# A hybrid convolution and attention block on eight cores: output rounds of two tiles, a block finish dealt by step, a later first stage, one jump to each body

## The chip, the cores and the metric

The kernel runs on the eight cores of one Trainium2 chip, as one program without collectives. Each core has its own engines (TensorE, VectorE or DVE, ScalarE or ACT, GpSimd or POOL, SyncE or SP) and DMA queues. The metric is the device time in microseconds of the slowest core. Cores 0 to 3 take one sequence of the batch and cores 4 to 7 the other; core c runs the code of piece c modulo 4.

## What is computed

```python
xn = rmsnorm(x, g_in)                                   # x: (2, 4096, 4096)
proj = xn @ w_in
gB, gC, h, z_conv, c_q, c_kv, k_rope, z_attn = split(proj)
y_conv = gB * causal_short_conv(gC * h, conv_w) * silu(z_conv)        # 2048 channels
q = rmsnorm(c_q) @ w_uq ; k_nope, v = split(rmsnorm(c_kv) @ w_ukv)    # 16 heads, 128 + 64 rotary
attn = chunk_causal_attention(q, k, v)                  # chunks of 64 frames, blocks of 128
y = concat(y_conv, attn * silu(z_attn))
out = rmsnorm(x + y @ w_out, g_final)
```

## The kernel before

`build_core` writes the instruction lists of one piece of the sequence. `PLAN` gives each piece its start, its number of tokens and their groups: piece 0 has 1232 tokens in groups of 360, 360 and 512, piece 1 has 1072 (280, 280, 512), piece 2 has 944 (432, 512), piece 3 has 848 (464, 384). A later piece has fewer tokens but more keys before it. Each piece is held transposed, features on partitions, in `XG` (bf16). `Prog.add` records each instruction with what it reads and writes and puts in the semaphore waits; on each engine the instructions run in the order in which the code records them. So code that stands earlier runs earlier on its engine, and an instruction that waits holds up everything behind it on that engine or DMA queue.

`emit_all` writes the four bodies one behind the other, each inside `with eng.If(place == k)`. An engine of piece 2 branches past the bodies of pieces 0 and 1 before its own and past that of piece 3 afterwards.

The stages, in order, with the lines by which they are known in the profile:

- First stage (L575, L582, L593): the first 12 weight tiles (j) of the input projection, while x is still being loaded. It goes in passes over feature tiles 0 to 4, 4 to 12, 12 to 20 and 20 to 32 (`PASSES`; pieces with two groups split the last 20 in another way). A unit is one tile j over one stretch of a pass: an fp32 piece is loaded into `ust` (`load_u`, sync queue), multiplied by the norm's gain into `uw` in bf16 by DVE (`make_u`, L503), and used by 3 or 2 matmuls for each feature tile. The first J = 8 // NG units of a pass run side by side in the banks of PSUM, the others one by one. `make_u(u + NU - 1)` at the start of a stretch scales all units for which there is a buffer (NU is 7 on piece 0). After each unit and group `keep` copies the bank to `Pb` or `Pz` (L519, L517) or adds it (L515). `squares(c)` squares four feature tiles on ACT and adds them up on DVE, in one go. `load_x` starts the x loads on POOL's queue, four feature tiles each, at the units that `xs` names; each waits for the scaling of its unit.
- Projections of the remaining columns with the convolution (L649), the compressed keys (L765, L766), queries (L869) and gates (L889).
- Attention (L948 to L1221): 16 heads, each with SP_ steps of two key tiles for one token group (10 steps on piece 0, where the blocks of groups 0, 1 and 2 have 2, 3 and 5 steps). A step x has: scores of step x + 1 (`qk`), Exp on ACT, projection units of the next head (banks 6 and 7 in turn), mask and sum on DVE, some parts of the finish of the block before, and the product with V (L1221). `finish_block` returns seven parts: ls = sum, lhi = bf16 of it, llo = rest, `sums` (two matmuls with ones, L1055 and L1056), `inverse` (Ln and Exp on ACT), rl = rl * gate (L1066), G = bank * rl (L1067). In each step `npop` parts are taken, 7 divided by the steps of the block, rounded up: 4, 3 or 2 for piece 0.
- Output stage, first groups (L1137): all groups but the last, features on partitions. For each of 8 column tiles ct of 512 and each of 8 weight pieces kg (4 feature tiles x 512 columns, bf16, from the copy `wbf`), the four feature tiles dt are computed, in `abank(ct, dt, g)`: with two groups of tokens (GA == 2) that is all eight banks. Then `evac_a` (L1276 to L1284) adds the residual `XA` (two buffers; `load_ra(dt_ + 2)` follows the copy) into `HA`, squares it and adds up the squares. Before the first round a part of it is put off (`late`, `done`), since the banks are still used by attention. `EB` and `early_at` put 28 matmuls of the first tile into the last head.
- Output stage, last group (L1345): tokens on partitions, weights as moving operand, 8 column tiles of 512, `bbank` in turn. `norm_a` (L1327, L1328) sums the squares of the first groups by two matmuls after the second weight piece; `out_a` and `out_b` scale and store.

The weight pieces come through a ring of NW `WO` buffers; `woload(i)` loads piece i on the sync queue when piece i - NW has been used.

## Time and profile before

| | us |
|---|---|
| median of 3 runs | 2929.17 |
| lowest and highest of them | 2682.77, 3073.19 |
| the profiled execution | 2686.84 |
| its span, core 0 (the slowest) | 2685.2 |
| spans of cores 1, 2, 3 | 2639.5, 2560.0, 2584.3 |
| spans of cores 4, 5, 6, 7 | 2672.5, 2639.7, 2563.5, 2590.1 |
| core 0: TensorE busy, weight loads busy | 2507.9, 1411.8 |
| core 0: DVE, ACT, POOL busy | 1264.1, 412.7, 55.5 |

The profile is one execution, recorded by the hardware. A row of a timeline has the start in microseconds from the span's start, the time taken, the engine, the line of the kernel, the operation, what it writes and reads, and in brackets how long the engine stood idle before it and who released it. PE is TensorE's matmuls, PEld its weight loads. The granted clock is 1.00 at 2.4 GHz and 0.50 at 1.2 GHz; a share between is a mean over a stretch. A DMA share is the mean busy share of the core's 16 DMA engines.

### The profile page before, as it was taken

Reading aid. Unit: us, or ns where it says so; the run is one execution under the profiler, and the core shown is the slowest. Engines: PE = TensorE matmul, PEld = TensorE weight load, DVE = VectorE, ACT = ScalarE, POOL = GpSimd, SP = SyncE. Lnnn points to the kernel's source line nnn. Section 1 sums busy time; section 2 is a strip of 40 time slices with the busy share of each in tenths; the row PEclk is TensorE's granted clock in tenths of the full one; section 3 lists DMA queues with packets and bytes.
Section 4 is the critical chain, followed back from the end, with each engine's and each line's share of the span. In section 5 each row is a group of like instructions: output and inputs, shape, how many; then the busy total and the mean of one; then the engine's idle time right before and its main releaser. Section 6 shows DMA issues by size and latency. Waiting matters only on the chain.

```text
span 2685.2 us, 37379 instructions; the slowest of 8 cores (2560.0 to 2685.2 us)
## 1 busy us (share of the span) xinstructions
PE 2507.9 (93%) x14462; PEld 1411.8 (53%) x14630; DVE 1264.1 (47%) x1953; ACT 412.7 (15%) x739; POOL 55.5 (2%) x103
## 2 busy tenths in 40 slices
PE   5899999999999999999999999888888989899996
PEld 3445555555555555555555555454544555554442
DVE  3767666444454444443354334777776021215213
ACT  1210000000000000010011003444444000001102
POOL 0000000000000000000000001111100000000000
PEclk7899999999999999999999999999999999899998
DMA  8832544444444444412435456999831443438965
GB/s 174 208 101 72 161 135 144 139 148 148 148 148 148 153 144 131 137 53 64 126 95 157 125 121 115 152 147 129 127 74 59 132 131 118 129 116 280 312 202 173
DMA packets 118363, 374.32 MB, mean 139 GB/s; under 512 B 13456, under 2 KB 18960, under 8 KB 118032
## 3 DMA queue, kind: packets, MB, share of 16 engines
q1 hardware_dynamic: 98784, 311.18, 37.8%
q0 software_dynamic: 17072, 56.25, 13.6%
q10 hardware_dynamic: 2304, 4.20, 0.4%
q8 instruction: 125, 2.05, 0.3%
q14 instruction: 78, 0.64, 0.1%
HBM read 402.59 MB, written 58.79 MB: 172 GB/s over the span
## 4 chain that ended last, share of the span: by engine, by line
PE 87%; DVE 4%; DMA 3%; issue 2%; ACT 2%; SPq 0%; ACTq 0%; DVEq 0%
PE ps L649 32%; PE ps L1137 11%; PE ps L889 10%; PE ps L1345 7%; PE ps L593 6%; PE ps L869 5%; PE ps L948 5%; PE ps L765 2%; PE ps L1221 1%; PE ps L1038 1%; PE ps L1039 1%; DMA XA_a<-x_own 1%; PE ps L958 1%; PE ps L968 1%; DMA ust_a<-w_in_t 1%
## 5 line engine op out<-in xcount | busy, mean ns | idle before, releaser
L649 PE MATMUL ps<-XG_a,ws_a 128*128 128x360 bf16 (+2 forms) x4940 | 865.0, 337 | 2.7
L649 PEld LDWEIGHTS ps<-XG_a,ws_a 128*128 128x128 bf16 x4992 | 488.3, 98 | 379.2
L438 DVE TENSOR_TENSOR ws_a<-stg_a,g_in_a 128x1024 bf16<-128x1024 f32 x304 | 358.2, 1219 | 175.6 <-DMA stg_a<-w_in_t 175.5
L889 PE MATMUL ps<-XG_a,ws_a 128*128 128x360 bf16 (+1 forms) x1521 | 266.4, 337 | 1.0 <-issue 0.2
L889 PEld LDWEIGHTS ps<-XG_a,ws_a 128*128 128x128 bf16 x1536 | 150.2, 98 | 116.7 <-issue 0.3
L1137 PE MATMUL ps<-YA_a,WO_a 128*128 128x360 bf16 x1024 | 178.0, 338 | 31.5 <-DVE HA_a L1276 31.5
L593 PE MATMUL ps<-XG_a,uw_a 128*128 128x360 bf16 (+1 forms) x944 | 178.3, 351 | 30.3 <-DVE Pb_a L519 16.5
L948 PE MATMUL ps<-CQG_a,WQ_a 128*128 128x360 bf16 (+1 forms) x757 | 153.0, 354 | 11.0 <-DVE QN_a L951 10.6
L1137 PEld LDWEIGHTS ps<-YA_a,WO_a 128*128 128x128 bf16 x1024 | 104.6, 103 | 102.9 <-issue 44.3
L1276 DVE TENSOR_TENSOR HA_a<-ps,XA_a 128x720 f32<-128x720 f32 x32 | 28.9, 905 | 274.3 <-PE ps L1137 247.7
L1137 PE MATMUL ps<-G_a,WO_a 128*128 128x360 bf16 x1024 | 158.0, 316 | 0.0
L593 PEld LDWEIGHTS ps<-XG_a,uw_a 128*128 128x128 bf16 x960 | 96.8, 101 | 111.4 <-issue 40.3
L869 PE MATMUL ps<-XG_a,ws_a 128*128 128x360 bf16 (+1 forms) x767 | 137.0, 337 | 0.4
L1137 PEld LDWEIGHTS ps<-G_a,WO_a 128*128 128x128 bf16 x1024 | 100.1, 98 | 55.9
L948 PEld LDWEIGHTS ps<-CQG_a,WQ_a 128*128 128x128 bf16 x768 | 77.1, 103 | 71.8 <-issue 14.9
L1345 PE MATMUL ps<-WO_a,G_a 128*128 128x512 bf16 x500 | 113.7, 384 | 0.6
L1345 PE MATMUL ps<-WO_a,YB_a 128*128 128x512 bf16 x503 | 111.8, 379 | 0.5
L869 PEld LDWEIGHTS ps<-XG_a,ws_a 128*128 128x128 bf16 x768 | 75.0, 98 | 57.9
L1038 PE MATMUL ps<-QN_a,KH_a 128*128 128x512 bf16 (+7 forms) x303 | 95.8, 325 | 0.2
L1039 PE MATMUL ps<-TQ_a,K_a 128*128 128x512 bf16 (+6 forms) x299 | 91.1, 325 | 0.1
L1345 PEld LDWEIGHTS ps<-WO_a,G_a 128*128 128x128 bf16 x512 | 50.7, 99 | 62.0 <-issue 3.3
L1358 DVE TENSOR_TENSOR HB_a<-ps,XR_a 128x512 f32<-128x512 f32 x32 | 22.1, 691 | 128.4 <-PE ps L1345 128.2
(158 smaller groups left out, 2076.5 us busy)
## 6 DMA issues: line engine op xcount, KB each, us to landing
stg_a<-w_in_t SPq DMA_DIRECT2D x304, 512.0 KB, 5.5
WO_a<-wbf SPq DMA_DIRECT2D x128, 512.0 KB, 4.1
wbf<-w_out_t POOLq DMA_DIRECT2D x64, 512.0 KB, 16.8
ust_a<-w_in_t SPq DMA_DIRECT2D x36, 512.0 KB, 5.0
XA_a<-x_own SPq DMA_DIRECT2D x32, 360.0 KB, 4.6
outA<-HA_a SPq DMA_DIRECT2D x32, 360.0 KB, 6.5
wst_a<-w_ckv SPq DMA_DIRECT2D x16, 576.0 KB, 5.5
XG_a<-x_own POOLq DMA_DIRECT2D x7, 1232.0 KB, 20.0
```

The lines of the kernel that those rows point to most:

```text
L438: tt(WS[i % 2][:, 8 * c:8 * c + 8, :], stg[q % 3][:, :, :], gains(8, 8 * c, 128), ALU.mult)
L593: mm(o, uw[(u + g_) % NU][:, kc - k0, :], xk(kc, g), kc == k_start, kc == k_end - 1)
L649: mm(o, w[:, kc, :], XG[:, kc, c0:c1], kc == 0, kc == 31)
L765: mm(psum[0:wd, A, :], x_, WC[:, kc, 0:512], kc == 0, kc == 31)
L869: mm(o, w[:, kc, :], xk(kc, g), kc == 0, kc == 31)
L889: mm(o, w[:, kc, :], xk(kc, g), kc == 0, kc == 31)
L948: mm(o, WQ[h % 2][:, kc, part * 128:(part + 1) * 128], CQG[:, kc, a:b], kc == 0, kc == 7)
L1038: mm(o, KH[h % 2][:, j * 128:j * 128 + 128], QN[h % 2][:, a + off:b], True, False)
L1039: mm(o, K2[:, j * 128:j * 128 + 128], TQ[h % 2][:, a + off:b], False, True)
L1137: mm(psum[:, abank(ct, dt, g), 0:b - a], WO[slot][:, kcc, dt * 128:(dt + 1) * 128], src, kc == 0, kc == 31)
L1276: tt(v, psum[:, b0:b0 + 2, 0:gA], XA[dt_ % 2][:, :].rearrange("p (g t) -> p g t", g=2), ALU.add)
L1345: mm(bank(bbank(ct, t_)), src, WO[slot][:, kcc, :], kc == 16, kc == 15)
```

## The change

The bodies are reached by a chain of compares and one jump, and lie in the order of pieces 3, 0, 1, 2; each ends with one jump to the end, announced by a hint. In the first stage all pieces use the four passes of piece 0; only the units that the next products need are scaled ahead; the parts of `squares` are queued and taken one to three at a time behind `keep` (`ease`); x comes in pairs of feature tiles; weight units 2 to 4 wait for x tile 0, and those behind them for x tile 1. In attention each part of the finish has a step at which it is due, by the steps of the block that runs then. In the output stage a round makes two feature tiles, with a new layout of `wbf` (a piece has 8 feature tiles x 256 columns), and the last group's pieces are put together from two halves.

```diff
 def emit_all(progs, place_d, nc, stack):
     def run_all(ename, eng):
         place = eng.value_load(place_d)
-        for k, P in enumerate(progs):
-            with eng.If(place == k):
-                run(P, ename, eng)
...
+        eng.br(tests[0])
+        for k in range(n - 1):
+            with nc.body(tests[k], valid_engines=only):
+                eng.br_eq(place, k, bodies[k], tests[k + 1] if k < n - 2 else bodies[n - 1])
+        for k in [n - 1] + list(range(n - 1)):
+            with nc.body(bodies[k], valid_engines=only):
+                ahead = eng.mark_branch_hint_location()
+                run(progs[k], ename, eng)
+                eng.br(ename + "_done").branch_hint(ahead)
+        nc.switch_bb(ename + "_done")
...
-    if NG == 3:
-        PASSES = (((0, 4),), ((4, 12),), ((12, 20),), ((20, 24), (24, 32)))
-    else:
-        PASSES = (((0, 4),), ((4, 12),), ((12, 16), (16, 24), (24, 32)))
+    PASSES = (((0, 4),), ((4, 12),), ((12, 20),), ((20, 24), (24, 32)))
...
+    def ease(m):
+        for _ in range(m):
+            if sqq:
+                sqq.pop(0)()
...
-    xs = {-1: ((0, 1), (1, 2), (2, 4)), 0: ((4, 8),), 3: ((8, 12),), 7: ((12, 16),), 11: ((16, 20),), 15: ((20, 24),),
-          18: ((24, 28),), 21: ((28, 32),)}
+    xs = {-1: ((0, 1), (1, 2), (2, 4)), 36: ()}
+    for i, at in enumerate((2, 4, 6, 8, 13, 15, 17, 19, 24, 26, 28, 30, 32, 34)):
+        xs[at] = ((4 + 2 * i, 6 + 2 * i),)
...
-    for u in range(4):
+    for u in range(2):
         load_u(u)
+    for u in range(2, 5):
+        load_u(u, [XG[:, 0, 32:34]])
...
-    for u in range(4, NU):
-        load_u(u)
+    for u in range(5, NU):
+        load_u(u, [XG[:, 1, 32:34]])
...
-            make_u(u + NU - 1)
+            make_u(u + J - 1)
...
+                make_u(u + J + len(pieces) - 1)
...
+                        ease(1 if p < NP - 1 else 2)
...
-                        make_u(u + g_ + NU - 4)
+                        make_u(u + g_ + len(pieces))
...
+                ease(1 if p < NP - 1 else 3)
...
+    def abank(r, d, g):
+        return (6 + GA * (2 * r + d) + g) % 8
+
+    def a_mm(r, kg, d, g):
         a, b = GRP[g]
+        w = WO[(4 * r + kg // 2) % NW]
...
+    def spread(x):
+        c = sum(1 for q in per if q[0] == per[(x + 1) % SP_][0])
+        return (range(7) if c > 6 else (0, 0, 1, 2, 2, 3, 4) if c > 4 else (0, 0, 1, 2, 2, 3, 3) if c > 3 else (0, 0, 0, 1, 1, 2, 2))
...
-        npop = -(-7 // max(1, sum(1 for q in per if q[0] == g)))
-        for _ in range(npop):
-            if slow:
-                slow.pop(0)()
+        while slow and slow[0][0] <= x:
+            slow.pop(0)[1]()
...
+            behind.append(lambda h=h, g=g, gb=gb, x=x: slow.extend(
+                zip([x + 1 + q for q in spread(x)], finish_block(h, g, gb))))
...
+    for r in range(16):
+        for kg in range(8):
+            for d in range(2):
+                for g in range(GA):
+                    if r > 0 or (kg, d, g) not in early:
+                        a_mm(r, kg, d, g)
+                if slow and kg > 0:
+                    slow.pop(0)[1]()
+            if kg % 2:
+                woload(4 * r + kg // 2 + NW)
+        for d in range(2):
+            evac_a(r, d)
```

Three places show how the change moves instructions on piece 0. The numbers in the names only tell buffers apart. The lines of the changed kernel are other numbers for the same statements.

DVE at the start of the first stage, before the change (the scaling of units 3 to 6 and the first copies out of PSUM):

```order
L503 TENSOR_TENSOR uw3_a_95<-ust3_a_88,g_in_a_43 128x512
L503 TENSOR_TENSOR uw4_a_96<-ust4_a_89,g_in_a_43 128x512
L503 TENSOR_TENSOR uw5_a_97<-ust5_a_90,g_in_a_43 128x512
L503 TENSOR_TENSOR uw6_a_98<-ust6_a_91,g_in_a_43 128x512
L519 COPY Pb_0_a_73<-ps 128x360
L519 COPY Pb_0_a_73<-ps 128x512
L519 COPY Pz_0_a_74<-ps 128x360
L519 COPY Pz_0_a_74<-ps 128x512
```

and with it (from unit 0 on):

```order
L511 TENSOR_TENSOR uw0_a_92<-ust0_a_85,g_in_a_43 128x512
L511 TENSOR_TENSOR uw1_a_93<-ust1_a_86,g_in_a_43 128x512
L511 TENSOR_TENSOR uw2_a_94<-ust2_a_87,g_in_a_43 128x512
L527 COPY Pb_0_a_73<-ps 128x360
L527 COPY Pb_0_a_73<-ps 128x512
L527 COPY Pz_0_a_74<-ps 128x360
L527 COPY Pz_0_a_74<-ps 128x512
L511 TENSOR_TENSOR uw3_a_95<-ust3_a_88,g_in_a_43 128x512
```

The copies of the first units stood behind the scalings of seven units, and now stand behind three.

TensorE in attention, where the block of group 2 (512 tokens) has ended and the next head's group 0 begins, before (L948 a projection unit, L1055 and L1056 the sums, L1221 the product with V, L1038 and L1039 scores):

```order
L948 MATMUL ps<-CQG_a_125,WQ1_a_152 128x360 x16
L1055 MATMUL ps<-lhi_a_149,ones16_a_47 128x512
L1056 MATMUL ps<-llo_a_150,ones16_a_47 128x512
L1221 MATMUL ps<-PT0_a_141,VH1_a_136 128x360
L1221 MATMUL ps<-PT0_a_141,VH1_a_136 128x232
L1038 MATMUL ps<-QN0_a_137,KH0_a_133 128x360
L1039 MATMUL ps<-TQ0_a_139,K2_a_72 128x360
L1038 MATMUL ps<-QN0_a_137,KH0_a_133 128x360
L1039 MATMUL ps<-TQ0_a_139,K2_a_72 128x360
L948 MATMUL ps<-CQG_a_125,WQ1_a_152 128x360 x8
```

and with the change (L977, L1084 and L1085, L1250, L1067 and L1068):

```order
L977 MATMUL ps<-CQG_a_125,WQ1_a_152 128x360 x16
L1250 MATMUL ps<-PT0_a_141,VH1_a_136 128x360
L1250 MATMUL ps<-PT0_a_141,VH1_a_136 128x232
L1067 MATMUL ps<-QN0_a_137,KH0_a_133 128x360
L1068 MATMUL ps<-TQ0_a_139,K2_a_72 128x360
L1067 MATMUL ps<-QN0_a_137,KH0_a_133 128x360
L1068 MATMUL ps<-TQ0_a_139,K2_a_72 128x360
L977 MATMUL ps<-CQG_a_125,WQ1_a_152 128x360 x8
L1084 MATMUL ps<-lhi_a_149,ones16_a_47 128x512
L1085 MATMUL ps<-llo_a_150,ones16_a_47 128x512
L1250 MATMUL ps<-PT1_a_142,VH1_a_136 128x104
```

The two sum matmuls have moved one step on, behind a product with V, four score matmuls and eight matmuls of a unit.

The sync queue in the output stage, at the end of the first round (WO are weight pieces, XA residuals), before:

```order
L385 DMA WO4_a_160<-wbf 128x2048
L385 DMA WO5_a_161<-wbf 128x2048
L385 DMA WO6_a_162<-wbf 128x2048
L385 DMA WO7_a_163<-wbf 128x2048
L385 DMA XA0_a_167<-x_own 128x720
L385 DMA XA1_a_168<-x_own 128x720
L385 DMA XA0_a_167<-x_own 128x720
L385 DMA XA1_a_168<-x_own 128x720
L385 DMA WO8_a_164<-wbf 128x2048
L385 DMA WO0_a_156<-wbf 128x2048
```

and with the change, from the first round to the third:

```order
L396 DMA WO0_a_156<-wbf 128x2048
L396 DMA WO1_a_157<-wbf 128x2048
L396 DMA WO2_a_158<-wbf 128x2048
L396 DMA WO3_a_159<-wbf 128x2048
L396 DMA XA0_a_167<-x_own 128x720
L396 DMA XA1_a_168<-x_own 128x720
L396 DMA WO4_a_160<-wbf 128x2048
L396 DMA WO5_a_161<-wbf 128x2048
L396 DMA WO6_a_162<-wbf 128x2048
L396 DMA WO7_a_163<-wbf 128x2048
```

Four residual loads stood together behind eight weight loads; now two of them follow each four.

## Rows read from the trace of the kernel before

**Rows 1.** List of cores: span and mean granted TensorE clock.

```profile
core 0: 2685.2 us, clock 0.967
core 1: 2639.5 us, clock 0.981
core 7: 2590.1 us, clock 0.993
```

**Rows 2.** Table by stage, core 0: length, five engines' busy us, clock, DMA, GB/s.

```profile
0.00:272.00 272.00, 223.55 (x1219) 123.52 (x1241) 171.56 (x237) 43.82 (x34) 7.88 (x15) 0.89 0.56 140
1224.00:1362.00 138.00, 137.58 (x797) 78.05 (x804) 49.71 (x66) 12.68 (x26) 0.00 (x0) 1.00 0.35 107
1651.00:2053.00 402.00, 342.53 (x2047) 199.50 (x2078) 285.88 (x693) 185.00 (x390) 42.37 (x78) 0.95 0.76 118
2070.00:2430.00 360.00, 328.15 (x2025) 202.48 (x2027) 56.22 (x69) 24.51 (x31) 0.00 (x0) 0.94 0.40 123
2430.00:2660.00 230.00, 223.57 (x1007) 101.00 (x1026) 84.81 (x128) 35.11 (x81) 0.00 (x0) 0.99 0.76 256
```

**Rows 3.** Table by stage, core 1: first stage and output stage.

```profile
0.00:241.00 241.00, 196.46 (x1238) 123.55 (x1239) 158.85 (x236) 38.62 (x34) 7.86 (x15) 0.93 0.60 152
2094.00:2386.00 292.00, 258.83 (x2023) 203.09 (x2024) 45.92 (x67) 20.65 (x31) 0.00 (x0) 0.94 0.47 143
```

**Rows 4.** Table by stage, core 7: first stage in part and whole, query projection.

```profile
30.00:90.00 60.00, 42.83 (x204) 20.67 (x205) 36.01 (x51) 17.67 (x21) 3.70 (x5) 0.86 1.03 239
0.00:199.40 199.40, 153.70 (x851) 82.50 (x852) 120.32 (x164) 32.84 (x33) 7.89 (x15) 0.95 0.70 177
1070.80:1165.50 94.70, 94.70 (x540) 52.00 (x539) 44.68 (x55) 9.16 (x19) 0.00 (x0) 1.00 0.52 156
```

**Rows 5.** Chain that ended last, core 0, output stage.

```profile
2115.25 38.04 PE ps L1137 x232
2153.76 4.18 DMA XA_a<-x_own
```

**Rows 6.** Chain that ended last, core 0, query projection.

```profile
1224.16 4.88 PE ps L869 x32
```

**Rows 7.** Waits of TensorE, core 0, output: total us, times, longest.

```profile
PE ps L1137 <- DVE HA_a L1276: 31.5, 14, 4.3
```

**Rows 8.** Waits of TensorE, core 7, from 30 us on.

```profile
PE ps L1327 <- DVE loA_d L1334: 6.8, 1, 6.8
```

**Rows 9.** Groups of the page, core 0: the output stage's copy.

```profile
L1276 DVE TENSOR_TENSOR HA_a<-ps,XA_a 128x720 f32<-128x720 f32 x32 | 28.9, 905 | 274.3 <-PE ps L1137 247.7
```

**Rows 10.** Waits of TensorE, core 0, attention.

```profile
PE ps L1056 <- DVE llo_a L1064: 23.3, 16, 3.1
PE ps L1055 <- DVE lhi_a L1063: 13.5, 7, 3.1
```

**Rows 11.** Timeline, core 0, first stage: start, us, instruction, idle before.

```profile
28.93 0.69 DVE L503 TENSOR_TENSOR uw_a<-ust_a,g_in_a 128x512 bf16<-128x512 f32 x1 [12.79 <-DMA ust_a<-w_in_t]
36.98 1.36 PE L593 MATMUL ps<-XG_a,uw_a 128*128 128x360 bf16 x4 [14.08 <-DVE Pb_a L519]
61.24 1.22 DVE L503 TENSOR_TENSOR uw_a<-ust_a,g_in_a 128x1024 bf16<-128x1024 f32 x1
```

**Rows 12.** DMA issues, core 0: KB each, median us to landing.

```profile
XG_a<-x_own POOLq DMA_DIRECT2D x2, 308.0 KB, 6.2
```

**Rows 13.** Timeline, cores 0, 1 and 7: DVE's first instruction.

```profile
2.79 0.17 DVE L378 MEMSET ones_a<- 128x128 bf16 x1 [2.79 <-issue]
6.72 0.17 DVE L378 MEMSET ones_b<- 128x128 bf16 x1 [6.72 <-issue]
17.89 0.17 DVE L378 MEMSET ones_d<- 128x128 bf16 x1 [17.89 <-issue]
```

**Rows 14.** Timeline, cores 0 and 7: the last store issued.

```profile
2669.96 1.35 ACTq L1389 DMA_DIRECT2D outB<-HB_a  x1
2586.59 0.34 ACTq L1389 DMA_DIRECT2D outB<-HB_d  x1
```

106 lines of the change are left out of this document (38 added, 68 removed).

## Prediction

> **What bounds the kernel now.** I read the list of cores first: each core holds one of four pieces of the sequence, and the run lasts as long as the slowest. Core 0 (piece 0, three token groups) sets the end with 2685.2 us; core 1 (piece 1) follows 46 us behind and core 7 (piece 3, two groups) 95 us behind [rows 1]. So the edits count first on core 0, and only until another core ends last.
>
> Next the table by stage for core 0. TensorE is the engine with the work; the question is what it loses. In the first stage it is busy 223.6 of 272 us at a granted clock of 0.89, in attention 342.5 of 402 us at 0.95, in the token-last output stage 328.2 of 360 us at 0.94; between them (1224:1362) it is busy 137.6 of 138 at 1.00 [rows 2]. Core 1 shows the same losses in its first and output stages [rows 3]. Core 7's last rows lie closer together: 153.7 of 199.4 us busy in the first stage, at a DMA share of 0.70 over the stage and of 1.03 in 30:90 [rows 4].
>
> **Output stage in rounds of two tiles.** Today a round makes four feature tiles, two banks each, so it fills all eight banks of three-group pieces. The next round waits until DVE has copied them out, and tiles three and four wait for residual loads that are issued only after copies one and two: in the chain 38.0 us of matmuls, 4.2 us of a load, and so on round by round [rows 5]. With two tiles per round four banks are always free and each residual load gets a whole round (some 19 us) instead of 4. All of the waiting should go. Clean pace: 32 matmuls of 360 columns in 4.88 us, 0.1525 each [rows 6]. The stage has 8 x 8 x 4 x 4 x 2 = 2048, of which 28 are done early: 2020 x 0.1525 = 308 us against 360, so 51 us less after a microsecond of start. The list of waits names 31.5 us of it [rows 7]; the rest is the clock, at its lower level after each wait. Core 1: 292 us, of which 33 idle and about 0.06 x 292 = 17 by the clock [rows 3], the two overlapping a little: 46 us. Core 7 uses one bank per tile, was already double-buffered and gains nothing here.
>
> The Trainium skill ("TensorE: Matmul & The Clock Gate", section "Loop structure matters more than you think") says that a DVE copy out of PSUM between tiles doesn't break the warmth of the array. The trace speaks against it where the copies are waited for: the stage's clock is 0.94 and its gaps are about 4 us. By that rule only the idle 32 us would come back and core 0 would lie 19 us higher, still not last.
>
> The final copy-out shrinks too: four tiles at the end become two, and the norm's sum matmul, which stands 32 matmuls (7 us) behind, waited 6.8 us for it on core 7 [rows 8]. Two tiles less are two copies of 0.9 us on core 0 [rows 9] with two sums of the same size and ACT's squares between them, some 5 us. I take the wait and the clock's dip behind it as gone: 8 us on cores 0 and 7, 6 on core 1; at least 3.
>
> **Block finish dealt by step.** Today the sum matmuls of a block stand on TensorE right behind the three DVE operations that feed them; now mostly a step later, and what follows them a step later again. TensorE's waits for them are 23.3 + 13.5 = 37 us in attention on core 0 [rows 10]. The idle total is 59.5 us, the other 22 stay and the clock costs up to 0.05 x 402 = 20 us [rows 2]. DVE's work is unchanged, 285.9 us, and would be 81% of a stage of 355 us, so some of it comes back: I take 37 - 10 for the waits and all 20 of the clock, since the longest waits (3.1 us), which are these, are what it can fall after. 47 us less; bounds 0 (DVE sets the pace) and 80 (nothing left idle). The blocks of cores 1 and 7 are longer; I count nothing there.
>
> **First stage.** Three edits with one aim. (a) Two units are scaled ahead of the first products instead of all buffers; today DVE stands 12.8 us before a late weight piece with finished banks behind it, and TensorE 14.1 us before DVE [rows 11]. (b) x comes in pairs of feature tiles spread over the units, weights 2 to 6 only behind the first x tiles. (c) The square sums go out in small parts between copies. Clean price on core 0: 1152 matmuls at the pace of the query projection, 768 wide ones (and 24 sums) in 137.6 us [rows 2], 206 us, against 272: 66 lost. DMA needs 0.56 x 272 = 152 us [rows 2], so it can hide. After: 14 us to the first product (a start at 6.7, see below, and a landing of 6.2 us [rows 12] or a little more), 206 of work, 10 until the start has caught up, 7 for the rest: 237, 35 less. Core 1 likewise 32. New cost: at the head of a pass the units 2 (three groups) or 2 to 4 (two groups) are scaled only after the last copy of the pass before, 1.22 us each [rows 11]. That is one unit, about 1.3 us, three times on core 0, and three units, about 3.3 us net, three times on core 7. Core 7: 768 matmuls at 94.7/512 = 0.185 are 142 us; its DMA needs 0.70 x 199.4 = 140 us [rows 4], nearly as much, so it can't be hidden fully. First product at 9 us, + 142 + 10 for pass heads + 6 for the front + 7 of DMA and small waits = 174, against 199.4: 25 less. Bounds: 12 (it keeps its 171 us from first product to end, and gets only the earlier start) and 40.
>
> **One jump.** The engines of cores 0, 1 and 7 begin at 2.8, 6.7 and 17.9 us [rows 13]: each body passed costs 4 to 6 us. At the end the last store is issued 13.9 us (core 0, 2671.3 to 2685.2) and 3.2 us (core 7, 2586.9 to 2590.1) before the end [rows 1, 14], 3.6 per body still to be passed. Now piece 3's body comes first and the others are one far jump away: core 0 begins 3.9 us later, core 7 15 us earlier (both are in the first-stage sums), and all end 3 to 4 us after the last issue: core 0 gains 10, core 1 7, core 7 nothing.
>
> The Trainium skill ("Advanced Engine Details and Errata", section "Control Flow Timing") gives 51 ns for a branch and 108 ns for a compare-and-branch. By these the bodies would cost nothing and core 7 could not gain 15 us; the starts in the trace contradict it. Its page "Runtime: NRT & Kernel Launch" (section "Instruction fetch mechanics") says that a far target stalls for its fetch, which fits them.
>
> Two prices no row shows. Weight pieces of the last stage are now two runs of 256 columns per chunk, 2 KB each in memory. As moving operand I take that at nothing (there is no gap inside a run, and 360 and 512 columns cost in proportion); the DMA share there is 0.76 [rows 2], room for longer packets.
>
> **Sum.** Core 0: 2685.2 - 51 - 8 - 47 - 35 - 10 = 2534. Core 1: 2639.5 - 46 - 6 - 32 - 7 = 2548. Core 7: 2590.1 - 25 - 8 = 2557. Core 7 now ends last. The profiled execution took 2686.84 us, 1.6 above its longest span: 2559, forecast 2560 us. The three runs shown spread from 2682.8 to 3073.2 with a median of 2929.17; the profiled one is at their lower end, and the forecast is for executions like it.
>
> **Rivals.**
> 1. Attention doesn't speed up, as DVE (71% busy, uneven over a head) sets its pace. For it: the later parts leave DVE as many operations in the same steps, and the copy of a unit now stands behind two more of them. Against it: the named waits are long and of one kind. Core 0: 2534 + 47 = 2581, time 2583.
> 2. The first stage is bound by DMA and by the new late scalings, not by order. For it: a DMA share above 1 in 30:90 on core 7. Against it: only 140 us of transfers in all. Core 7 then gains 0 to 12 us, and cores 0 and 1 nothing: 2569 to 2582, time 2571 to 2592, say 2585.
> 3. The rounds don't remove the gap, because the residual loads sit in the sync queue behind weight loads that wait for TensorE. For it: one queue in order. Against it: the loads come right behind the copies they wait for. Core 0: 2534 + 51 = 2585, time 2587.
> 4. Slower than before: the split moving operand halves the rate of the last stage's 1024 matmuls (now 223.6 us busy for 1007 of them, 0.22 each [rows 2]), 0.22 x 1024 = 225 us more, 2785. It decides from 0.12 us per matmul. Nothing in the trace speaks for it but that no such operand occurs.
>
> **How the numbers follow.** Forecast 0.62; rivals 0.11, 0.14, 0.05 and 0.04; several of 1 to 3 together, up to 2645 and so within 2%, 0.04. The forecast's spread is some 20 us, by the bounds of attention and of core 7's first stage; the range 2538 to 2602 takes in the first three rivals. Faster by over 2% (below 2633; 2% is about what a measurement of this kernel can tell from no change): 0.62 + 0.11 + 0.14 + 0.05 = 0.92. Within 2%: 0.04. Slower: 0.04.
>
> **What would show it.** Right: no wait of L1137's successor for HA, clock 1.00 through that stage, about 308 us long on core 0; waits for lhi/llo below 8 us and an attention stage near 355 us; engines of cores 3 and 7 starting near 3 us, of cores 0 to 2 and 4 to 6 near 6.7; core 7's first stage ending near 174 us; cores 3 and 7 last. Wrong: a DVE or clock share in attention as before, first-stage DMA shares of 1 with TensorE idle past 60 us, a last stage longer than 230 us.

## The result and the profile after

The changed kernel takes 2598.4 us (median of 4 executions, 2597.4 to 2782.3). The ratio to the kernel before on the same chip is 0.968, 95% interval 0.965 to 0.971: faster by 3.2%. The forecast was 2560, with the range up to 2602: the direction was right, but of the forecast gain of 127 us only 89 came. In some executions of either kernel the cores of one half of the chip, or of both, are disturbed and the time goes up to 3073 us; ratios, spans and means below leave such cores out. The profiled execution took 2598.04 us.

The list of cores after, against [rows 1]; core 4 holds the same piece as core 0:

```profile
core 0: 2596.1 us, clock 0.992
core 1: 2564.6 us, clock 0.993
core 4: 2596.4 us, clock 0.990
core 7: 2573.5 us, clock 0.992
```

Core 0 still ends last, with core 4; core 7, which was to end last, is 23 us ahead. Cutting the spans at the first projection product, the first and the last output matmul of attention and the last matmul of each output stage gives the account (us; forecast in brackets). "Attention" is here from the first to the last output matmul:

| | core 0 before | after | change | core 1 | core 7 |
|---|---|---|---|---|---|
| first stage | 271.5 | 259.1 | -12.4 (-35) | -11.4 (-32) | -5.3 (-25) |
| up to attention | 1375.2 | 1375.1 | -0.1 (0) | -2.0 (0) | -7.4 (0) |
| attention | 423.7 | 416.6 | -7.1 (-47) | +5.4 (0) | +0.6 (0) |
| output, rounds | 359.2 | 309.7 | -49.5 (-51) | -49.3 (-46) | +3.0 (0) |
| last stage | 230.0 | 221.6 | -8.4 (-8) | -6.6 (-6) | -8.5 (-8) |
| behind the last matmul | 25.6 | 14.0 | -11.6 (-10) | -11.0 (-7) | +1.0 (0) |
| span | 2685.2 | 2596.1 | -89.1 (-151) | -74.9 (-91) | -16.6 (-33) |

Three terms came within 2 us on core 0; the two others brought 19.5 of 82. (Of the 7.4 us of core 7 between the stages, 5.6 are nine waits for the scaled weights of the projection in the execution before; core 3, with the same code, took 7 us less there and has none of these waits.)

Each column is one execution, and core 0's "before" is a long one. Core 4, the same code in the same two executions, went from 2672.5 to 2596.4 us: its first stage gained 8.6 us and its attention only 1.2 (417.8 to 416.6), its rounds 47.7 and its last stage 6.5. Over the executions of the kernel before that ran beside the experiments, the spans of cores 0 and 4 have a mean of 2674 us (92 spans, 2661 to 2703), and with the change 2595 us (18 spans, 2591 to 2597).

The table by stage for core 0, against [rows 2] (length, busy us of TensorE, of its weight loads, VectorE, ScalarE, GpSimd, clock, DMA share, GB/s), says how:

```profile
0.00:259.00 259.00, 219.29 (x1236) 120.27 (x1237) 169.29 (x236) 43.72 (x34) 12.56 (x22) 0.95 0.59 147
1638.00:2035.00 397.00, 336.67 (x2096) 192.84 (x2094) 285.96 (x701) 185.89 (x395) 41.95 (x78) 1.00 0.78 122
2051.00:2360.00 309.00, 308.00 (x2019) 197.28 (x2017) 57.38 (x70) 25.31 (x32) 0.00 (x0) 1.00 0.48 143
2361.00:2582.00 221.00, 221.00 (x1027) 100.29 (x1025) 82.36 (x125) 33.58 (x80) 0.00 (x0) 1.00 0.82 263
```

The two output stages are full, 308 of 309 and 221 of 221 us at clock 1.00. Attention is idle for 60.3 of 397 us, against 59.5 of 402: the idle time did not fall at all. The first stage still lacks 40 us.

The chain that ended last on core 0 is, from the stage's start to the end of the window asked (2130 us), one piece of matmuls, where [rows 5] had a load after every 232. The copy's group on the page (of core 4) answers to [rows 9]: the same 32 copies of 904 ns. The lines between the two are all waits of TensorE on core 0 from 2051 to 2582 us, both output stages: they are for the last block's sums, and no wait for HA, 31.5 us before [rows 7], is left.

```profile
2055.21 74.88 PE ps L1166 x491
```

```profile
PE ps L1084 <- DVE lhi_a L1092: 0.6, 1, 0.6
PE ps L1085 <- DVE llo_a L1093: 0.4, 1, 0.4
```

```profile
L1307 DVE TENSOR_TENSOR HA_a<-ps,XA_a 128x720 f32<-128x720 f32 x32 | 28.9, 904 | 217.6 <-PE ps L1166 217.6
L1353 PE MATMUL ps<-WO_a,G_a 128*128 128x512 bf16 x512 | 112.5, 379 | 0.0
```

The second line of this pair is the last stage with the split moving operand: no idle time before it, and 221.00 busy us for 1027 records, 0.215 each, against 0.222 before [rows 2]. Rival 4 is gone.

TensorE's waits in the attention of core 0 (total us, times, longest), against [rows 10]:

```profile
PE ps L1250 <- DVE G_a L1096: 17.6, 16, 1.9
PE ps L997 <- ACT VH_a L998: 13.3, 7, 1.9
PE ps L997 <- ACT KH_a L988: 11.8, 7, 1.7
PE ps L1084 <- DVE TQ_a L980: 11.0, 13, 0.8
PE ps L1084 <- DVE lhi_a L1092: 1.0, 1, 1.0
```

The waits for lhi and llo are gone, as forecast (below 8 us). In their place stand an output matmul (L1250) that needs the bank of the block before last (G), units (L997) that need a bank still being copied by ScalarE, and sum matmuls (L1084) that need a bank still being copied by VectorE.

TensorE's waits in the first stage, of core 0 from its first product on (the one of 6.2 us for x is the one before that product) and then of core 7:

```profile
PE ps L620 <- DVE uw_a L511: 8.9, 6, 3.4
PE ps L600 <- DMA XG_a<-x_own: 8.3, 3, 6.2
PE ps L620 <- DVE Pz_a L523: 7.3, 2, 4.0
PE ps L600 <- DVE uw_a L511: 3.6, 3, 1.6
```

```profile
PE ps L620 <- DVE uw_d L511: 15.1, 6, 6.4
PE ps L600 <- DVE uw_d L511: 12.0, 8, 3.1
PE ps L620 <- DVE hsq_d L632: 4.4, 1, 4.4
```

On core 7, 27 us are waits for scaled weights. Its longest, from the timeline (VectorE, VectorE, TensorE):

```profile
149.32 1.04 DVE L544 TENSOR_TENSOR sq_d<-sq_d,sq_d 128x1696 bf16<-128x1696 bf16 x1 [2.85 <-ACT sq_d L535]
153.96 1.82 DVE L511 TENSOR_TENSOR uw_d<-ust_d,g_in_d 128x512 bf16<-128x512 f32 x2
154.79 0.55 PE L620 MATMUL ps<-XG_d,uw_d 128*128 128x464 bf16 x1 [6.38 <-DVE uw_d L511]
```

VectorE stood 2.85 us before a part of the square sums (edit c), which needs ScalarE's squares, then did four copies and two more parts, and only then the scaling that TensorE waited for. The timeline also shows the start (POOL's first x load and TensorE's first product on core 0, then VectorE's first instruction on cores 0 and 7, [rows 13]):

```profile
10.21 1.92 POOL L396 DMA_DIRECT2D XG_a<-x_own  x3 [9.51 <-issue]
19.34 1.19 PE L600 MATMUL ps<-XG_a,uw_a 128*128 128x360 bf16 x3 [6.20 <-DMA XG_a<-x_own]
```

```profile
6.90 0.17 DVE L389 MEMSET ones_a<- 128x128 bf16 x1 [6.90 <-issue]
2.90 0.17 DVE L389 MEMSET ones_d<- 128x128 bf16 x1 [2.90 <-issue]
```

### The profile page after: what moved, and what is told of

It is laid out like the page before. It is cut to its first block, busy times and chain, and to the rows that moved or that the text cites. A ratio compares the mean times of both kernels' runs of the same rounds, so it can differ in the third digit from the quotient of the medians.

```text
span 2596.4 us, 37267 instructions; the slowest of 8 cores (2564.1 to 2596.4 us)
## 1 busy us (share of the span) xinstructions
PE 2472.4 (95%) x14487; PEld 1397.7 (54%) x14630; DVE 1259.5 (49%) x1953; ACT 410.6 (16%) x739; POOL 59.6 (2%) x110
## 4 chain that ended last, share of the span: by engine, by line
PE 89%; DVE 4%; ACT 3%; issue 3%; DMA 1%; ACTq 0%; DVEq 0%; POOLq 0%; POOL 0%; SPq 0%
PE ps L678 33%; PE ps L1166 12%; PE ps L918 9%; PE ps L1353 7%; PE ps L620 6%; PE ps L898 5%; PE ps L977 4%; PE ps L794 3%; PE ps L1250 2%; PE ps L997 1%; PE ps L987 1%; PE ps L1068 1%; PE ps L1067 1%; PE ps L600 1%; ACT rl_a L1088 1%
## 5 line engine op out<-in xcount | busy, mean ns | idle before, releaser
L1166 PE MATMUL ps<-YA_a,WO_a 128*128 128x360 bf16 x1024 | 160.2, 317 | 0.0
L977 PE MATMUL ps<-CQG_a,WQ_a 128*128 128x360 bf16 (+1 forms) x765 | 144.3, 337 | 0.7
L977 PEld LDWEIGHTS ps<-CQG_a,WQ_a 128*128 128x128 bf16 x768 | 72.3, 98 | 56.8 <-issue 5.4
L1250 PE MATMUL ps<-PT_a,VH_a 128*128 128x512 bf16 (+7 forms) x302 | 71.4, 311 | 21.8 <-DVE G_a L1096 17.6
L1067 PE MATMUL ps<-QN_a,KH_a 128*128 128x512 bf16 (+7 forms) x298 | 89.5, 310 | 0.1
L1068 PE MATMUL ps<-TQ_a,K_a 128*128 128x512 bf16 (+7 forms) x297 | 86.0, 310 | 0.3
```

The costliest lines, as they stand in the source:

```text
L977: mm(o, WQ[h % 2][:, kc, part * 128:(part + 1) * 128], CQG[:, kc, a:b], kc == 0, kc == 7)
L1067: mm(o, KH[h % 2][:, j * 128:j * 128 + 128], QN[h % 2][:, a + off:b], True, False)
L1068: mm(o, K2[:, j * 128:j * 128 + 128], TQ[h % 2][:, a + off:b], False, True)
L1166: mm(psum[:, abank(r, d, g), 0:b - a], w[:, c:c + 128], src, kc == 0, kc == 31)
L1250: mm(psum[:, 4 + gb % 2, off:w], VH[(h // 2) % 2][:, j, (h % 2) * 128:(h % 2) * 128 + 128], pt[:, p_, off:w], first and p_ == 0, last and ...
```

## The experiments

All but rounds_only and jump_only start from the changed kernel. What each theory expected was written before the run. Edits (b) and (c) of the first stage were not run alone.

**First stage undone.**

```diff
-    PASSES = (((0, 4),), ((4, 12),), ((12, 20),), ((20, 24), (24, 32)))
+    if NG == 3:
+        PASSES = (((0, 4),), ((4, 12),), ((12, 20),), ((20, 24), (24, 32)))
+    else:
+        PASSES = (((0, 4),), ((4, 12),), ((12, 16), (16, 24), (24, 32)))
...
-            make_u(u + J - 1)
+            make_u(u + NU - 1)
...
```

(also x's loads, the weight loads and the squares as before)

> The changed kernel with the first stage of the kernel before (passes, weight scaling ahead by all buffers, x in fours, squares at once); the rest stays changed. Theory A (the late scaling behind all copies of the first units costs the pieces with two groups what the earlier start gives them): core 0's first stage ends some 12 to 16 us later (about 273), core 2's some 18 us earlier (about 199 instead of 217.9), core 7's some 9 us earlier (about 185 instead of 194); slowest core 0, about 2610 us. Rival B (the stage is bound by DMA, so the order of scaling matters little): cores 2 and 7 end the stage within 4 us of 217.9 and 194.

Measured: two executions of 2625.07 (profiled) and 2618.51 us. Core 0 is at 2610.4 us; core 4, with the same code, ended last at 2623.5. The first stage ends at 273.3 us on core 0 (after 259.1), 241.4 on core 1 (229.4) and 181.9 on core 7 (194.0). So the new first stage is worth 14 and 12 us on the three-group pieces in this record, and costs the two-group piece 12. Cores 4 and 5 ended the stage later still, at 286.8 and 268.6 us: the old stage varies. The whole spans say 17 us for piece 0 (mean 2612.7 of seven spans, against 2595.3). What core 7 gained came from the jump alone.

**Scaling further ahead.**

```diff
-                make_u(u + J + len(pieces) - 1)
+                make_u(min(u + J + len(pieces) - 1 + (3 if p else 0), u + NU - 1))
-                        make_u(u + g_ + len(pieces))
+                        make_u(min(u + g_ + len(pieces) + (3 if p else max(0, j - 2 * NF + 4)), u + NU - 1))
```

> The changed kernel, but from the second pass on each unit is scaled three units earlier than now (three more before the copies of the first units of a pass). x loads keep their units. Theory A (late scaling costs): TensorE's waits for uw on cores 2 and 7 (27 us each) fall below 8 us, their first stage ends 18 to 25 us earlier, core 0's 8 to 12 us earlier; slowest core 0 at about 2587 us. Rival B (DMA): the waits stay as waits for loads, the first stage ends less than 5 us earlier on all cores, 2594 us or more.

Measured: ratio 0.971 (0.967 to 0.975), as the changed kernel. First stage: core 7 at 180.7 us, 13 sooner; core 0 at 262.9, 4 later. Both theories missed: the gain on core 7 is below the 18 to 25 of theory A (its waits for scaled weights fell from 27 to 13 us, not below 8, and one of 11.6 us for the squares came up), and core 0 lost instead of winning 8 to 12. TensorE's waits on core 0:

```profile
PE ps L600 <- DVE uw_a L511: 6.5, 1, 6.5
PE ps L620 <- DVE Pz_a L523: 6.4, 3, 3.2
PE ps L600 <- DVE Pz_a L527: 6.0, 1, 6.0
```

Of core 0's 4 us, 3 lie before its first product (22.3 against 19.3 us), so this record alone does not show what the larger lead cost; but cores 0 and 4 ended at a mean of 2599.1 us over seven spans, 4 later than with the change. The timeline shows the way (VectorE, then TensorE):

```profile
63.93 1.23 DVE L511 TENSOR_TENSOR uw_a<-ust_a,g_in_a 128x1024 bf16<-128x1024 f32 x1 [3.77 <-DMA XG_a<-x_own]
65.75 0.46 PE L600 MATMUL ps<-XG_a,uw_a 128*128 128x360 bf16 x1 [6.02 <-DVE Pz_a L527]
```

Where three units are scaled ahead, VectorE again stands before a late load with finished banks behind it, and TensorE waits for their copies; where one is, TensorE waits for the scaling. On core 0 the second is the smaller evil; on core 7 the first. The small lead suits core 0 and was given to both.

**The body order.**

```diff
-        eng.br(tests[0])
-        for k in range(n - 1):
+        eng.br(tests[1])
+        for k in range(1, n):
...
-        for k in [n - 1] + list(range(n - 1)):
+        for k in range(n):
```

> The changed kernel with the four bodies in the order of pieces 0, 1, 2, 3: piece 0's body is the one that the chain of tests falls into. After the change core 0 issues its first x load at 10.2 us, before it at 3.2, and its first product stands at 19.3 us. Theory: a body reached by a far jump costs 4 us on SP, DVE and TensorE and 7 on POOL, and the cost lands on the core that ends last. Core 0 then issues x at 3.2 us, has its first product at 9 to 12 us instead of 19.3, its first stage ends 5 to 9 us earlier (250 to 254 instead of 259.1), and the time is 2590 to 2593 us, against 2598. Cores 3 and 7 start near 7 us and end 4 to 8 us later, at 2575 to 2580, still not last. Rival: the first stage absorbs the start, as the later weight pieces and the scalings set its end; it ends at 258 to 260 and the time is 2597 to 2599.

Measured: three executions of 2584.6 to 2590.3 us, ratio 0.966 (0.963 to 0.968); core 0 at 2583.0, core 7 at 2578.6. Core 0's timeline:

```profile
3.29 1.91 POOL L396 DMA_DIRECT2D XG_a<-x_own  x3 [2.59 <-issue]
8.79 0.47 PE L600 MATMUL ps<-XG_a,uw_a 128*128 128x360 bf16 x2
```

The first product comes 10.5 us sooner and the stage ends at 244.7 us, 14.4 sooner: more than the theory's 5 to 9. (The granted clock fits the other 4: it was 0.81 in the first 40 us of the changed kernel and 1.00 in the first 26 here.) The span is 13 us shorter, and 11 by the means of seven spans of cores 0 and 4 (2584.6) and of the change. Cores 3 and 7 lose 9 and 5 us. Rival "absorbed" falls. The forecast had priced the far body at 3.9 us; it cost core 0, the slowest, 14 in its first stage: POOL issued x 7 us later, and from there to the first product it took 9.1 us instead of 5.5 (why the landing was slower is open).

**One jump alone on the kernel before.**

```diff
-        for k, P in enumerate(progs):
-            with eng.If(place == k):
-                run(P, ename, eng)
+        only = [eng.engine]
+        n = len(progs)
...
+                eng.br(ename + "_done").branch_hint(ahead)
+        nc.switch_bb(ename + "_done")
```

> The kernel before with the one jump alone. Prediction's theory: core 0 begins 4 us later and ends 10 us sooner behind its last store, core 1 ends 7 us sooner, core 7 begins 15 us sooner. With the first stage of before the late start of core 0 should be absorbed by the wait for x that follows (first products at 9 us were followed by a wait to 18.6), so core 0 ends 6 to 10 us sooner, at 2675 to 2679, and core 7 12 to 16 us sooner, at 2574 to 2578; the ratio is 0.996 to 0.998. Rival: POOL's 7 us later x load is paid in full, and core 0 gains 0 to 3 us only, ratio 0.999 to 1.000.

Measured: ratio 0.997 (0.995 to 1.000); core 0 at 2667.7 us in the profiled execution, core 7 at 2563.8. Behind the last matmul core 0 gains 11.1 us, as it does after the change. Its first stage ends at 268.5 us, 3 sooner in spite of a first product at 19.1 us instead of 9.2; but core 4, its twin, ends the stage at 276.1 us, 8 later than before. So that the old order hides the late start behind its long waits is not shown by these records. The spans say more: cores 0 and 4 have a mean of 2666.7 us over 15 spans, against 2673 before on the same chip (24 spans), 6.5 sooner. That is nearer to the first theory (6 to 10) than to the rival (0 to 3), though single spans scatter by 6 to 7 us; of the 11 us gained at the end some 4 or 5 are lost on the way, where the new first stage loses 14 (the experiment before). The interval of the ratio does not tell the two theories apart. Core 7 gains 26 us, more than its start of 15: its first stage alone gains 19, and 9 lie between the stages, in the loss named under the table.

**The output rounds alone on the kernel before.** (the changed output stage, all else as before)

```diff
-    for ct in range(8):
+    for r in range(16):
+        for kg in range(8):
+            for d in range(2):
...
```

> The kernel before with the output stage in rounds of two tiles alone (its first stage, its dealing of the finish and its four conditional bodies kept). Prediction's terms: 51 us in the rounds and 8 at the last copy-out on core 0, 46 and 6 on core 1, 8 on core 7. If they stand alone and add: core 0 2685 - 59 = 2626, ratio 0.977 to 0.980, TensorE's waits for HA gone and the clock 1.00 in the stage. Rival: part of the 51 came from the other edits (the queue order, an earlier start): ratio 0.983 or above.

Measured: profiled execution 2621.8 us, core 0 at 2620.2; the other undisturbed execution took 2641.3. The table of the stage on core 0:

```profile
2064.00:2373.40 309.40, 308.44 (x2023) 197.54 (x2025) 57.77 (x69) 25.30 (x32) 0.00 (x0) 1.00 0.47 143
```

The rounds take 309.3 us (before 359.2) and the last stage 221.5 (230.0): 49.9 and 8.5 us, the same as in the whole change (core 4 has the same 309.3 and 221.6). The two terms stand alone and add. The first stage of this execution ended 6 us sooner than before's, the rest of the gain, and is no effect of this edit. On core 7, where the forecast was 0, the rounds take 3 us more.

**The dealing of the finish undone.**

```diff
-        while slow and slow[0][0] <= x:
-            slow.pop(0)[1]()
+        npop = -(-7 // max(1, sum(1 for q in per if q[0] == g)))
+        for _ in range(npop):
+            if slow:
+                slow.pop(0)[1]()
```

> The changed kernel with the block finish dealt as before (7 parts divided by the steps of the block). Theory A (the new dealing takes away the waits for the sums and puts new ones in their place): core 0's attention some 7 us longer (441 instead of 434), core 1's 5 us shorter (588 instead of 593), slowest core 0 at about 2605 us. Rival B (the dealing gave the whole clock loss back and something else in the changed kernel took it): core 0's attention 20 us or more longer, 2616 us or more.

Measured: ratio 0.970 (0.966 to 0.974), core 0 at 2598.8 us. Attention takes 420.9 us on core 0, 4.3 more than after, and 566.0 on core 1, 5.1 less. The waits are those of before again:

```profile
PE ps L1084 <- DVE lhi_a L1092: 26.9, 15, 3.1
PE ps L977 <- DVE QN_a L980: 10.0, 7, 1.7
PE ps L987 <- DVE TQ_a L980: 9.7, 7, 1.4
```

So 32.2 of 33.6 us of waits for lhi and llo went by the dealing, and 4.3 us of core 0's attention. Even these 4.3 are much: core 4, with 36.6 us of the same waits, needs 417.9 us in this run, 1.3 more than after, and the spans of cores 0 and 4 differ by 1.5 us (mean 2596.8 over nine spans against 2595.3). With the old dealing attention took 416.1 to 423.7 us on these two cores in four kernels, with the new one 416.5 to 417.2. The dealing is worth some 1 to 4 us on piece 0 and costs piece 1 five. The table over attention, of before, of this kernel and of the change:

```profile
1647.00:2070.00 423.00, 362.48 (x2154) 210.38 (x2188) 301.27 (x732) 195.94 (x411) 42.37 (x78) 0.95 0.75 120
```

```profile
1634.00:2054.00 420.00, 364.08 (x2189) 208.67 (x2186) 300.85 (x732) 195.68 (x411) 42.63 (x78) 0.96 0.78 121
```

```profile
1634.00:2051.00 417.00, 354.25 (x2196) 202.45 (x2195) 298.89 (x736) 194.10 (x413) 41.95 (x78) 0.99 0.77 123
```

TensorE's busy time fell from 364.1 to 354.3 us as the granted clock rose from 0.96 to 0.99, and its idle time rose from 55.9 to 62.8. The small gain is all clock: 10 us won there, 7 given back in new waits. (The longest wait is now 1.9 us, it was 3.1; no run changed that length alone, so that the clock rose for this reason is not shown.)

**Blocks of one or two steps finished a step earlier.**

```diff
-        return (range(7) if c > 6 else (0, 0, 1, 2, 2, 3, 4) if c > 4 else (0, 0, 1, 2, 2, 3, 3) if c > 3 else (0, 0, 0, 1, 1, 2, 2))
+        return (range(7) if c > 6 else (0, 0, 1, 2, 2, 3, 4) if c > 4 else (0, 0, 1, 2, 2, 3, 3) if c > 3 else (0, 0, 0, 1, 1, 2, 2) if c > 2 else (0, 0, 0, 1, 1, 1, 1))
```

> The changed kernel, but where the block that runs has two steps, the last four parts of the finish all come in its second step (0,0,0,1,1,1,1). Theory A (TensorE waits 17.6 us in all, 16 times, for the last part of the finish, since the third block writes the same PSUM bank): this wait goes and core 0's attention is 10 to 16 us shorter, about 2584 us. Rival B (DVE sets the pace over the head, and the wait moves to another place): attention 0 to 4 us shorter, 2592 to 2598 us.

Measured: ratio 0.986 (0.982 to 0.991), core 0 at 2637.9 us, attention 458.3 us: 42 more. A clear miss. The wait for G is gone, and in its place:

```profile
PE ps L977 <- DVE QN_a L980: 38.4, 13, 3.0
```

The last two parts of a finish wait for ScalarE's inverse; put a step earlier they stand in VectorE's queue ahead of a unit's copy, and TensorE waits for that copy. (VectorE's own waits for the inverse rose from 12.6 to 21.3 us.) One step of position in a queue that runs in order is worth 42 us.

**The sums in the output bank.**

```diff
-            b_ = ubank() if sumbank[0] is None else sumbank[0]
+            b_ = 4 + gb % 2
```

> The changed kernel, but the sum matmuls of a finished block write into that block's own output bank (over its values, so that the output is not the reference's) instead of taking one of the two banks in which the units of the next head are made. After the change TensorE's waits in core 0's attention are 17.6 us for G, 13.3 for VH, 11.8 for KH, 11.0 for TQ, 61 in all, where before 37 of 59.5 were for the sums. Theory A: the later parts of a finish now hold a unit bank, or arrive when both are taken, so the units wait for their copies: the waits for VH, KH and TQ fall by 20 to 35 us together, the attention stage of core 0 from 434.5 to 400 to 415, time 2565 to 2580. Theory B: DVE and ACT, busy 286 and 186 of 397 us and loaded unevenly, set the pace of a head; a wait taken away at one instruction comes back at the next: attention 428 to 436, time 2591 to 2600.

Measured: 2579.5 us median, ratio 0.962 (0.960 to 0.964); core 0 at 2578.8, attention 398.1 us, 18.5 less. The waits for VH, KH and TQ are gone altogether; what comes up in their place:

```profile
PE ps L1250 <- DVE PT_a L389: 17.4, 49, 1.4
PE ps L1250 <- DVE G_a L1096: 14.6, 15, 1.9
```

Theory A holds in its mechanism, and comes out just under its size (20 us or more were expected): all 36 us of bank waits went, half of them were time, and 14 came back as waits for the zero fill of the next probabilities. The collision itself can be seen in the timeline of the changed kernel, TensorE first and then ScalarE in the same 5 us:

```profile
1809.23 1.04 PE L997 MATMUL ps<-WKV_a,CKVN_a 128*128 128x256 bf16 x8
1810.10 0.32 PE L1084 MATMUL ps<-lhi_a,ones_a 128*128 128x360 bf16 x1
...
1813.15 1.03 PE L997 MATMUL ps<-WKV_a,CKVN_a 128*128 128x256 bf16 x8 [1.90 <-ACT VH_a L998]
```

```profile
1810.66 0.47 ACT L1088 ACTIVATE rl_a<-ps 128x360 f32<-128x360 f32 x1 [1.43 <-PE ps L1085]
1811.23 0.50 ACT L1089 ACTIVATE rl_a<-rl_a 128x360 f32<-128x360 f32 x1
1811.64 0.88 ACT L1216 ACTIVATE PT_a<-ps 128x464 bf16<-128x464 f32 x2
1812.40 0.60 ACT L998 ACTIVATE VH_a<-ps 128x512 bf16<-128x512 f32 x1
```

A unit takes one of the two unit banks, the sums the other, and the next unit must have the first one again. Its copy (L998) could have begun when the unit's matmuls ended, near 1810.3, but ScalarE took the inverse and two exponentials first and began it at 1812.4.

**Less work for VectorE.**

```diff
-                lambda: tt(llo_, ls_, lhi_, ALU.subtract),
+                lambda: None,
...
-            mm(o[0], ones16[:, :], llo_, False, True)
+            mm(o[0], ones16[:, :], lhi_, False, True)
```

> The changed kernel without the subtraction that makes the low part of the block sums on DVE; the second sum matmul takes the high part again, so TensorE has the same work and the output is not the reference's. It takes 45 operations and some 20 us of work away from DVE in core 0's attention. Theory B (DVE's pace sets the stage): the stage gets 12 to 25 us shorter on core 0, 410 to 422, time 2574 to 2587. Theory A (bank rotation, not DVE's load): 0 to 5 us, time 2593 to 2599.

Measured: three executions of 2588.2 to 2591.9 us, ratio 0.966 (0.964 to 0.969); attention of core 0 407.8 us, 8.8 less. Between the theories: VectorE's load is part of it, not the pace.

**The sums in a score bank, full result.**

```diff
-            b_ = ubank() if sumbank[0] is None else sumbank[0]
+            b_ = 2 * (now[0] % 2) + 1 if sumbank[0] is None else sumbank[0]
...
-        return (range(7) if c > 6 else (0, 0, 1, 2, 2, 3, 4) if c > 4 else (0, 0, 1, 2, 2, 3, 3) if c > 3 else (0, 0, 0, 1, 1, 2, 2))
+        return ((0, 1, 2, 3, 3, 5, 6) if c > 6 else (0, 0, 1, 2, 2, 3, 4) if c > 4 else (0, 0, 1, 2, 2, 3, 3) if c > 3 else (0, 0, 0, 1, 1, 2, 2))
```

> The changed kernel; the sum matmuls of a finished block write into the score bank that the exponential of the same step has just read, instead of one of the two unit banks, and the inverse always follows in the same step. The result is the full one. The kernel with the sums in the output bank took 17 us off core 0's attention and the waits for VH, KH and TQ (36 us) with them. Theory A: what those units waited for was the bank, so the same 15 to 18 us go here too: attention of core 0 from 1634 to 2051 us becomes some 400 us long, time 2580 to 2583. Rival: the next score matmuls now wait for the inverse to read their bank (ACT comes late behind exponentials), which takes 5 to 20 us back: time 2585 to 2600, and the waits name L1067 or L1068 behind ACT's rl.

Measured: ratio 0.973 (0.969 to 0.977). Core 0 falls to 2578.5 us, attention 398.2, just as with the output bank; so the bank is what those 18 us were. But core 1 rises to 2593.1 and core 3 to 2599.3, and the time with them. TensorE's waits in the attention of core 1:

```profile
PE ps L1252 <- ACT PT_b L1214: 19.1, 37, 0.8
PE ps L1067 <- ACT rl_b L1089: 8.1, 31, 0.4
```

There the first was 11.5 us in the changed kernel and the second nil: the next scores now wait for the inverse. The rival was right, on cores that the expectation had not counted. (The waits explain some 16 of core 1's 27 us; the rest is open. For blocks of more than six steps this run also moved the inverse into the step of the sums; the two edits were not run apart.)

**The parts together.** piece0_first, sums_score, and the scaling three units ahead for two-group pieces only.

> Three things together on the changed kernel: piece 0's body reached by falling through (13 us on core 0), the sums in the score bank (17 us on core 0), and for the two-group pieces the scaling three units ahead from the second pass on (13 to 17 us on cores 2, 3, 6, 7). If they add: core 0 2583 - 17 = 2566, core 1 2571, core 7 2578 - 13 = 2565; core 1 ends last, time 2572 to 2575. If the sums' bank only moves waits: core 0 stays last at 2575 to 2583, time 2577 to 2585.

Measured: ratio 0.973 (0.970 to 0.977): core 0 at 2564.7 us, as the sum said, but core 1 at 2593.5 and core 3 at 2606.4. Both expected times (2572 to 2575, 2577 to 2585) were missed: the long pieces undo the gain. (Of core 3's time 20 us lie between the first stage and attention, 14.1 in waits for scaled weights of the projection; in the same execution core 7, with the same code, has no such waits and is at 2592.2.) Then the same with the score bank for piece 0 alone and the old dealing for piece 1:

```diff
+            b_ = sumbank[0] if sumbank[0] is not None else 2 * (now[0] % 2) + 1 if s0 == 0 else ubank()
...
+        if place == 1:
+            return [q // -(-7 // c) for q in range(7)]
```

> The kernel best, but with the sums in the score bank for piece 0 alone (its long-block pieces keep the unit banks), and with piece 1 dealing its finish as before the change (7 us less there). In sums_score core 0 gained 17.6 us, while cores 1, 3 and 7 got 19 to 31 us longer, as their next score matmuls and exponentials stand behind the inverse. If that is all: core 0 at 2565 to 2567, core 1 at 2564 to 2571, cores 3 and 7 at 2564 to 2572, time 2568 to 2574, ratio 0.957 to 0.962. Rival: cores 3 and 7 keep a loss by their later start and the scaling ahead (2580): time 2580 to 2584.

Measured: lowest 2572.9 us, ratio 0.961 (0.956 to 0.967), core 0 at 2566.9, core 7 at 2576.4. Without the subtraction on top of it:

> best2 without the subtraction of the low part on DVE (the second sum matmul takes the high part again; output not the reference's). Theory: with the bank free, DVE's load is what is left, and core 0's attention gets 10 to 18 us shorter than best2's. Rival: the rest is latency (exponential to memset to output matmul, sum to inverse to output): 0 to 6 us. The time itself is set by another core then; the stage on core 0 is what counts.

Measured: attention of core 0 392.5 us against 399.2, 6.7 less, just above the rival's 0 to 6 and below the theory's 10. What else the stage waits for was not tested. Since best2 had run on another chip than the change, both ran once more on one:

> The changed kernel once more, on the same chip as best2_again: ratio to the kernel before 0.965 to 0.971, core 0 and 4 last at 2595 to 2598, core 0's first stage ending at 256 to 261 us and its attention (first to last output matmul) 415 to 418 us.

> best2 once more, beside the changed kernel. If its gain is real: ratio 0.957 to 0.962, cores 3 and 7 last at 2571 to 2578, core 0 at 2565 to 2569, 18 to 26 us below the changed kernel. If it was the chip: both within 8 us of each other.

Measured: the changed kernel 2597.7 us, ratio 0.969 (0.965 to 0.973); best2 2572.0 us, ratio 0.960 (0.956 to 0.965), core 0 at 2570.5 and core 7 at 2568.7. best2 is 26 us faster than the change and 109 than the kernel before; the executions of the two do not overlap (2570.0 to 2583.8 and 2596.8 to 2597.8 us).

## Why the prediction was right in its direction and wrong in its size

**Output rounds (51): right.** 49.5 us on core 0 and 49.3 on core 1, alone and in the whole. The argument that the clock comes back too was needed: the idle 32 us alone would have left 18 us unexplained, and the stage now runs at a granted clock of 1.00 instead of 0.94. The Trainium skill ("TensorE: Matmul & The Clock Gate", "Loop structure matters more than you think") says that a copy out of PSUM does not break TensorE's warmth where the next matmuls follow immediately. Here they did not follow, but waited some 4 us for the copies [rows 7], and the clock was 0.94: the case lies outside that rule, and the prediction had taken it too wide.

**Last copy-out and norm (8): right,** 8.4 and 8.5 us. **Split operand (nothing): right.** **Jump at the end (10): right,** 11.6; on core 1 it was 11.0 for 7.

**Block finish (47, got 7 on core 0 and 1 on core 4; by the dealing 1 to 4): the step that failed.** It took "37 - 10 for the waits" from the names of the waits [rows 10]. They went, but the parts that were moved later landed elsewhere in the same head of 26 us: the sums on a unit bank between two units (18 us by sums_bank), the last parts against the output bank (17.6 us of waits for G) or, a step earlier, ahead of the copies of units (42 us, finish_two). The step priced the removed wait and gave ten for "DVE sets the pace"; but what a head lacked was first of all banks and places in three queues in order; 20 us less of VectorE's load gave 6.7 to 8.8. The clock's part, taken as 20 us, was 8 to 10. The bounds 0 and 80 held it; rival 1 had the right result by half the right reason (it named the unit's copy behind two more operations). On core 1 the step was put at nothing because its blocks are longer; there attention took 5.4 us more, 5.1 of them by the dealing (undo_finish).

**First stage (35, 32, 25; got 12, 11, 5): failed in three sub-steps.** The first product on core 0 came at 19.3, not 14 us: "a start at 6.7 and a landing of 6.2" used VectorE's start for all engines, where POOL, which loads x, came at 10.2. The "7 us for the rest" were 26 us of waits behind the first product: pass heads of up to 4.0 us (one price per head had been written, 1.3), and 12.5 us for scalings that were now just too late. With 19.3 us to the first product and the 206 of work they make 251 of the 259 us; the 8 left are for the clock, forecast at 10. On core 7 the stage got longer, 171 to 185 us from first product to end, past the bound that said it would at least keep its 171: the case that a smaller lead costs was priced at the heads alone, and the waits of 2.6 us at the heads are eight copies and three parts of the square sums in VectorE's queue before one scaling (54.7 to 61.2 us), the one of 6.4 us is a wait for ScalarE that edit (c) put in front of it.

**Jump at the start (in the 35): mis-sized.** Priced 4 us on core 0, it was 14 in the first stage, by piece0_first. The Trainium skill ("Runtime: NRT & Kernel Launch", "Instruction fetch mechanics") speaks of a stall while a far target is fetched. The trace agrees in that the start is late, by 4 us on VectorE and 7 on POOL; it does not show the fetch. The figures of the Trainium skill for the branches themselves ("Advanced Engine Details and Errata", "Control Flow Timing") are 51 and 108 ns and do not hold this delay.

**The sum.** Each core was summed rightly, but with two terms short on core 0 by 40 and 23 us and one on core 7 by 20, core 0 stayed last: 2534 + 40 + 23 = 2597. So the time lies inside the range by luck: it is 38 us above the forecast because core 7 was forecast last, at 2557, while core 0 missed its own sum by 62. What came is nearest to "several of 1 to 3 together", given 0.04. (The 2645 written there does not follow from its terms: all three give 2534 + 47 + 51 + 35 = 2667.) Both misses have one form: they priced an operation moved later by the wait that it left, and not by what it then stood behind or ahead of.

## What to carry to other kernels

A wait that fills a place may only be counted as gained where nothing else in the period is short. That held in the output stage (four free banks, whole rounds of slack: 51 forecast, 49.5 measured) and failed where two banks and three in-order queues carry a period of 26 us (32 us of named waits removed, 1 to 4 us gained). There, ask for every moved part which bank it holds and what stands behind it in its queue. And when the pieces of a kernel differ, the late piece should get the cheap place (here the body that is fallen into, 11 to 13 us), and a setting tuned for it should not be given to the others.

## What was not expected of the hardware

- A body reached by a far jump costs each engine another time: on core 0 VectorE began at 6.9 instead of 3.0 us, POOL issued its first load at 10.2 instead of 3.3. At the end every core issued its last store 4 to 5 us before its end, where the kernel before needed 3.6 us for each body passed.
- The same first stage ended at 271.5 and 265.6 us on core 0 in two kernels whose code up to there does not differ. On core 4 it ended at 267.7 and 269.2. In undo_first the old stage, reached by the jump, ended at 273.3 us on core 0 and 286.8 on core 4. Differences of 6 us in that stage of a single profiled execution tell nothing; the spans of several do.
- Waits of up to 4.3 us each, 32 us in all, cost the output stage another 18 us by the granted clock (0.94; 1.00 without them). With waits of at most 1.9 us attention was granted 0.99, and with waits of up to 3.1 us 0.96, at about the same idle time. Whether the length of the single wait decides was not tested.
